# Scoring three query blocks in one run, and turning the second attention's weighted sum

## The reference

```python
# first block, 8 heads, 16 meta tokens ahead of the 512; mask by chunks of 64 positions
s = einsum('bqhmd,bkhmd->bhmqk', q, k)              # two maps m per head, 64 features each
p = softmax(where(mask, s, NEG_INF))
a = p[:, :, 0] - lam * p[:, :, 1]
o = einsum('bhqk,bkhe->bqhe', a, v)                 # then rms norm, gate
# second block, dsa_attention, 4 heads of 64 features, 128 keys selected for each query
p = softmax(where(valid, einsum('bqhd,bqkhd->bqhk', q, ks) * scale, -inf))
hC = einsum('bqhk,bqkhd->bqhd', p, vs)
out = concatenate([hA, hB, hC]) @ w_out
```

## Time and profile before

| what | value |
|---|---|
| runs | 1533.29, 1533.55, 1533.76 us |
| profiled execution | 1534.0 us, span of its instructions 1532.1 us |
| TensorE busy | 1520.7 us, 9994 passes |
| VectorE, ScalarE, GpSimd busy | 1101.7, 646.7, 55.4 us |
| DMA | 131.64 MB, 86 GB/s on average |
| granted TensorE clock | 1.000 on average |

### The profile page before, as it was taken

How to read it: one execution, slowest core, us unless ns; L and a number is a source line. 1 busy time by engine, 2 the same in 40 slices (tenths; PEclk the granted TensorE clock), 3 DMA queues, 4 the chain that set the end, 5 groups by cost and what they waited for, 6 DMA issues and landing times.

```text
span 1532.1 us, 25451 instructions
## 1 busy us (share of the span) xinstructions
PE 1520.7 (99%) x9994; PEld 1362.9 (89%) x9994; DVE 1101.7 (72%) x1550; ACT 646.7 (42%) x1015; POOL 55.4 (4%) x115
## 2 busy tenths in 40 slices
PE   9999999999999999999999999999999999999998
PEld 8999999999999999999988888878888888888887
DVE  5889888888655587777764458988748887887123
ACT  5224545555643434434334335744645333333122
POOL 0000111111000000000000020000000000000000
PEclk9999999999999999999999999999999999999999
DMA  6333222232233243232232443231132333332221
GB/s 180 83 93 100 56 72 68 57 83 56 56 102 92 83 110 82 82 109 82 66 94 81 115 109 83 57 83 42 56 110 56 110 101 91 89 103 96 110 83 55
DMA packets 235360, 131.64 MB, mean 86 GB/s; under 512 B 20985, under 2 KB 228741, under 8 KB 235285
## 3 DMA queue, kind: packets, MB, share of 16 engines
q1 hardware_dynamic: 234900, 130.40, 30.3%
q0 software_dynamic: 384, 0.20, 0.0%
HBM read 128.48 MB, written 2.10 MB: 85 GB/s over the span
## 4 chain that ended last, share of the span: by engine, by line
PE 91%; DVE 5%; ACT 2%; issue 0%; DMA 0%; SPq 0%; DVEq 0%; ACTq 0%
PE psP L726 32%; PE psS L726 25%; PE psP L791 8%; PE psS L1432 4%; PE psP L1432 4%; PE psP L748 4%; PE psP L1122 3%; PE psP L1300 1%; DVE conv L2170 1%; PE psS L1300 1%; PE psP L969 1%; DVE wl L2050 1%; PE psP L879 1%; PE psS L928 1%; PE psS L1189 1%; PE psP L956 1%
## 5 line engine op out<-in xcount | busy, mean ns | idle before, releaser
L2050 DVE TENSOR_TENSOR wl<-raw,wh 128x2048 fp32r<-128x2048 f32 x124 | 284.1, 2291 | 174.8 <-ACT wh L1487 173.4
L1487 ACT ACTIVATE wh<-raw 128x2048 fp32r<-128x2048 f32 x124 | 237.0, 1911 | 207.1 <-PE psS L1432 74.3
L726 PE MATMUL psP<-xh,wh 128*128 128x264 f32 (+3 forms) x1184 | 296.0, 312 | 1.2 <-DVE wl L2050 0.5
L726 PE MATMUL psP<-xl,wh 128*128 128x264 f32 (+3 forms) x1184 | 291.4, 309 | 0.0
L726 PE MATMUL psP<-xh,wl 128*128 128x264 f32 (+3 forms) x1184 | 290.3, 308 | 0.0
L726 PE MATMUL psS<-xh,wh 128*128 128x256 f32 (+2 forms) x880 | 210.3, 305 | 0.4 <-DVE hT L2079 0.4
L726 PE MATMUL psS<-xl,wh 128*128 128x256 f32 (+2 forms) x880 | 208.1, 303 | 0.0
L726 PE MATMUL psS<-xh,wl 128*128 128x256 f32 (+2 forms) x880 | 207.2, 302 | 0.0
L726 PEld LDWEIGHTS psP<-xh,wh 128*128 128x128 f32 x1184 | 192.2, 189 | 16.3 <-issue 2.2
L726 PEld LDWEIGHTS psP<-xl,wh 128*128 128x128 f32 x1184 | 192.7, 189 | 12.0 <-issue 0.2
L726 PEld LDWEIGHTS psP<-xh,wl 128*128 128x128 f32 x1184 | 192.2, 189 | 11.9
(11 more groups left out here) (483 smaller groups left out, 2429.7 us busy)
## 6 DMA issues: line engine op xcount, KB each, us to landing
raw<-in_w_in_dram SPq DMA_DIRECT2D x74, 512.0 KB, 4.9
raw<-in_w_up_dram SPq DMA_DIRECT2D x44, 512.0 KB, 4.6
raw<-in_ffn_up_dram SPq DMA_DIRECT2D x44, 512.0 KB, 4.9
raw<-in_ffn_down_dram SPq DMA_DIRECT2D x22, 512.0 KB, 3.9
raw<-in_w_out_dram SPq DMA_DIRECT2D x16, 512.0 KB, 4.7
raw<-in_w_down_dram SPq DMA_DIRECT2D x16, 384.0 KB, 3.6
raw<-in_w_down_dram SPq DMA_DIRECT2D x16, 320.0 KB, 4.0
raw<-in_w_conv_out_dram SPq DMA_DIRECT2D x8, 512.0 KB, 4.6
```

The source lines that it names most:

```text
L726: ins = mm(dst, W[:, s, half, k, 0:rows], Y[:, k, c0 + o:c0 + o + w], start=(k == 0 and p == 0), stop=(k == KT - 1 and p == 2))
L1487: fn(wh[:, n % 2], raw[:, n % 2], ACT.Copy).then_inc(s_hi, 1)
L2050: V.tensor_tensor(wl[:, n % 2], raw[:, n % 2], wh[:, n % 2].bitcast(f32), ALU.subtract).then_inc(s_lo, 1)
```

## The change

First part, head stage. Blocks 0, 1 and 2 are scored one after another; blocks 0 and 1 share two PSUM banks (`SCORE_COL`), so maxima and exponentials of block 0 wait for block 1's scores and maxima. Turn-back goes to the front of the pass. Outputs (and VectorE's variances, ScalarE's output copy) go behind part 0 in passes 2 to 7, and stay ahead of it in passes 8 and 9. Values, scores 3 and the transposes of blocks 0 and 1 together (`first_probs`) stand behind part 1. ScalarE's and VectorE's orders follow.

Second part, second attention. ScalarE divides the probabilities in place (`divide_probs`) before they are transposed. `weighted` is made once a block, with the 64 value columns standing and 128 columns of turned probabilities moving, two heads in the two halves of the PSUM partitions; its result is already by feature, so `osb`, `scale_outputs` and `attention_back` go. High and low parts are taken block by block out of that bank.

```diff
+SCORE_COL = (0, 160, 0)
...
+        def score_rows(t):
+
+            o = SCORE_COL[t]
+            return scores_ps[:, 2 * (t // 2):2 * (t // 2) + 2, o:o + PW[t]]
...
             def scores(a, t):
-                if a:
-                    pe.wait_ge(s_ex, 4 * a + (0, 0, 1, 3)[t])
-                elif t >= 2:
-                    pe.wait_ge(s_ex, t - 1 if t == 2 else 3)
+                if t == 3:
+                    pe.wait_ge(s_ex, 4 * a + 3)
+                elif a:
+                    pe.wait_ge(s_ex, 4 * a)
...
+            def first_probs(a):
+                pe.wait_ge(s_cb, 4 * a + 2)
+                pe.wait_ge(s_ac, 4 * a + 1)
+                for j, o in enumerate((PO[0], PO[1], PO[1] + 128)):
+                    ins = tr(psP[1][:, 0, 128 * j:128 * (j + 1)], prob[:, o + NM:o + NM + 128], ident[:])
+                ins.then_inc(s_at, 1)
...
             for h in range(NH + 2):
                 a, b, c = h - 1, h - 2, h - 3
+                if c >= 0:
+                    pe.wait_ge(s_ea, evacuated(2 * (N_HEAD + 2 * h) - 2)[1])
+                    turn_back(c, psP[0])
                 if b >= 0:
                     probs(b, 3)
                 if 0 <= a < NH:
                     scores(a, 0)
                     scores(a, 1)
-                if c >= 0:
-                    pe.wait_ge(s_ea, evacuated(2 * (N_HEAD + 2 * h) - 2)[1])
-                    turn_back(c, psP[0])
-                if b >= 0:
+                    scores(a, 2)
+                if h >= NH:
                     outputs(b)
...
                 part(h, 0)
-                if 0 <= a < NH:
-                    if h < NH:
-                        values(a)
-                    scores(a, 2)
-                    probs(a, 0)
+                if 0 <= b < NH - 2:
+                    outputs(b)
...
                 part(h, 1)
                 if 0 <= a < NH:
-                    probs(a, 1)
+                    if h < NH:
+                        values(a)
                     scores(a, 3)
+                    first_probs(a)
                 part(h, 2)
...
-            def weighted(i, load, h0, h1):
+            def weighted(i, load):
...
-                for h in range(h0, h1):
-                    o = 256 * (i % 2) + 64 * h
+                for f in range(2):
+                    o = 256 * (i % 2) + 128 * f
                     for j in range(t + 1):
-                        ins = mm(psP[1][:, 1, o:o + 64], PT[:, h, 128 * j:128 * (j + 1)], av[:, j, 64 * h:64 * (h + 1)],
-                                 start=(j == 0), stop=(j == t))
+                        for b in range(2):
+                            h = 2 * f + b
+                            ins = mm(psP[1][64 * b:64 * b + 64, 1, o:o + 128], av[:, j, 64 * h:64 * (h + 1)],
+                                     PT[:, h, 128 * j:128 * (j + 1)], start=(j == 0), stop=(j == t))
+                ins.then_inc(s_po, 1)
...
             def exps(a, t):
-                act.wait_ge(s_ma, 4 * a + t + 1)
+                act.wait_ge(s_ma, 4 * a + max(t, 1) + 1)
...
-            def scale_outputs(i):
+            def divide_probs(i):
+                t = BLOCKS[i]
+                act.wait_ge(s_pn, i + 1)
+                for h in range(AT_H):
+                    p = prt[t][:, h, :]
+                    fn(p, p, ACT.Copy, scale=att[:, 1, i, h:h + 1]).then_inc(s_pw, 1)
...
             values(0)
             attention_exps(0)
             values(1)
+            divide_probs(0)
             hi(n + 13)
...
             attention_exps(2)
-            scale_outputs(1)
+            attention_hi(1)
+            divide_probs(2)
             copy_probs(2, 6, 0, 1)
             hi(N_WO2)
...
             copy_probs(2, 9, 3, 4)
+            divide_probs(3)
             gelu(2)
             lru_hi(1)
+            attention_hi(2)
             copy_probs(3, 10, 0, 4)
...
             for h in range(NH + 2):
                 n, a, b, c = N_HEAD + 2 * h, h - 1, h - 2, h - 3
+                if c >= 0:
+                    gated(c, psP[0])
                 if 0 <= a < NH:
                     maxima(a, 0)
                     maxima(a, 1)
...
-                if b >= 0:
+                if h >= NH:
                     variances(b)
+                if 0 <= a < NH:
+                    maxima(a, 2)
                 taps(2)
                 if h == NH:
                     dve.wait_ge(s_lmc, 1)
                     centred(0, 4)
-                if 0 <= a < NH:
-                    maxima(a, 2)
+                if 0 <= b < NH - 2:
+                    variances(b)
...
             mask_logits(0)
             select(3, 8, 10)
+            invert_sums(0)
             mask_logits(1)
-            invert_sums(0)
             lo(n + 13)
-            select(3, 10, 13)
+            select(3, 10, 12)
+            invert_sums(1)
+            select(3, 12, 13)
+            attention_lo(0)
             scaled(lg[:, 0, :], 2 * (n + 12))
```

More of the change, by code:

```diff
@@ L926, in scores @@
                     if t < 3:
-                        bank = scores_ps[:, 2 * (t % 2) + m, :]
-                        mm(bank[:, 0:PW[t]], q, K[:, 0:PW[t]], start=True, stop=False)
+                        bank = score_rows(t)[:, m, :]
+                        mm(bank, q, K[:, 0:PW[t]], start=True, stop=False)
                         last.append(bank[:, PW[t] - 64:PW[t]])
@@ L1364, in _ @@
             turn(0, 1, 2, 4)
-            weighted(0, 0, 0, 2)
             lru_side(0, 2, 4)
-            weighted(0, 1, 2, 4)
+            weighted(0, 1)
             lru_side(0, 4, 8)
@@ L1856, in copy_probs, with attention_hi @@
                 fn(PT[:, h0:h1, 0:w], psP[1][:, 0, 0:w * (h1 - h0)].rearrange("p (h c) -> p h c", c=w), ACT.Copy).then_inc(s_pc, 1)
-            def scale_outputs(i):
+            def divide_probs(i):
[4 more added lines that the diff above has]
+                    fn(p, p, ACT.Copy, scale=att[:, 1, i, h:h + 1]).then_inc(s_pw, 1)
+            def attention_hi(i):
                 t = BLOCKS[i]
                 act.wait_ge(s_po, i + 1)
-                act.wait_ge(s_pn, i + 1)
-                for h in range(AT_H):
-                    o = 256 * (i % 2) + 64 * h
-                    ins = fn(osb[:, t, 64 * h:64 * (h + 1)], psP[1][:, 1, o:o + 64], ACT.Copy, scale=att[:, 1, i, h:h + 1])
-                ins.then_inc(s_pd, 1)
+                o = 256 * (i % 2)
+                fn(ch[:, 6:8, 128 * t:128 * (t + 1)], psP[1][:, 1, o:o + 256].rearrange("p (f q) -> p f q", f=2), ACT.Copy).then_inc(s_hc, 1)
             def gelu(g):
@@ L1959, in _ @@
             attention_exps(1)
-            scale_outputs(0)
+            attention_hi(0)
+            divide_probs(1)
             copy_probs(1, 2, 0, 1)
@@ L1975, in _ @@
             copy_probs(2, 9, 3, 4)
+            divide_probs(3)
             gelu(2)
             lru_hi(1)
+            attention_hi(2)
             copy_probs(3, 10, 0, 4)
             lru_hi(2)
-            scale_outputs(2)
             hi(N_WO2 + 1)
-            scale_outputs(3)
-            act.wait_ge(s_pb, TT)
-            for f in range(2):
-                fn(ch[:, 6 + f, :], scores_ps[:, f, :], ACT.Copy).then_inc(s_hc, 1)
+            attention_hi(3)
             hi(N_WO2 + 2)
@@ L2260, in _ @@
                     maxima(a, 1)
-                if c >= 0:
-                    gated(c, psP[0])
-                if 0 <= a < NH:
                     ratios(a, 0, 2)
@@ L2674, in _, with attention_lo @@
                                        ch[:, g, :].bitcast(f32), ALU.mult, ALU.subtract).then_inc(s_hl, 1)
+            def attention_lo(i):
+                t = BLOCKS[i]
+                tok = slice(128 * t, 128 * (t + 1))
+                o = 256 * (i % 2)
+                dve.wait_ge(s_hc, i + 1)
+                V.tensor_tensor(cl[:, 6:8, tok], psP[1][:, 1, o:o + 256].rearrange("p (f q) -> p f q", f=2),
+                                ch[:, 6:8, tok].bitcast(f32), ALU.subtract).then_inc(s_hcl, 1)
             mask_logits(0)
             select(3, 8, 10)
+            invert_sums(0)
             mask_logits(1)
-            invert_sums(0)
             lo(n + 13)
-            select(3, 10, 13)
+            select(3, 10, 12)
+            invert_sums(1)
+            select(3, 12, 13)
+            attention_lo(0)
             scaled(lg[:, 0, :], 2 * (n + 12))
@@ L2683, in _ @@
             mask_logits(2)
-            invert_sums(1)
             scaled(lg[:, 1, :], 2 * (n + 12) + 1)
+            invert_sums(2)
+            attention_lo(1)
             mask_logits(3)
-            invert_sums(2)
             lo(N_WO2)
@@ L2695, in _ @@
             lru_lo(1)
+            attention_lo(2)
             lru_lo(2)
             lo(N_WO2 + 1)
-            for f in range(2):
-                dve.wait_ge(s_hc, f + 1)
-                V.tensor_tensor(cl[:, 6 + f, :], scores_ps[:, f, :], ch[:, 6 + f, :].bitcast(f32), ALU.subtract).then_inc(s_hcl, 1)
+            attention_lo(3)
             lo(N_WO2 + 2)
```

93 lines of the change are left out of this document (37 added, 56 removed).

## The result

The changed kernel takes 1538.2 us (median of 8 runs, 1536.9 to 1540.9); the kernel before took 1533.7 beside it (8 runs, 1533.3 to 1534.0). The ratio is 1.0031, 95% interval 1.0023 to 1.0040: slower by 4.5 us. Forecast: +3.4 us, 1537.0, with 0.56 on slower. The profiled execution took 1537.8 us, its span 1536.0.

What follows compares the result with a forecast made beforehand. TensorE, busy 1520.7 of 1532.1 us, was taken as the bound. Own work -5.5, first head's waits -0.3, eighth +3.5, ninth +0.6, second attention's waits +5.1 gave +3.4: 1537.0 us, range 1532.8 to 1540.6.

Steps and rivals of the forecast that it cites:

- Scores in one run: Heads: block 2's scores join a run already in paired form, gaining 0.27 us a head, 2.2 us over eight.
- Rival 4: Inner heads: VectorE's loop is longer than a head, six heads by 0.3 to 0.7: 1539 to 1541 us; chance 0.09.
- First, eighth and ninth: Heads with changed waits on TensorE: first head net -0.3 us, eighth +3.5, ninth pass +0.6.
- Second attention: Own work -0.9 for dropped turn-back and -2.4 for the weighted sum, waits +5.1; k = 2 comes 1.8 us later.
- The column halves: Second attention's weighted sum: the two halves overlap, 40 pairs at 0.11 us plus entries and exits, -2.4 us.
- four entries and exits: Second attention's weighted sum: entering and leaving the paired form four times, at about 0.35 us each.
- Rival 1: Second attention: column halves don't overlap, blocks 2 and 3 add 1.7 + 0.4: 1539.1 us; chance 0.22.
- 2 (waits covered): Eighth head and second attention: ScalarE's chain is not the last, so waits are covered: 1527.7 us, faster; chance 0.08.
- 3 (one stage only): Waits of either the eighth head or the attention are smaller by half or more: 1533 to 1535.3 us; chance 0.19.

Runs made afterwards that it cites:

- e1: The change's head-stage hunks only, with the second attention of the kernel before: 1536.3 us, ratio 1.0017.
- e4: Changed kernel plus 18 matmuls whose result nobody reads between parts 0 and 1 of the eighth head: 1538.0 us.
- e2: The change's second attention only, with the heads of the kernel before: 1536.2 us, ratio 1.0015.
- e6: As e3, but the weighted sum's two heads of a pair run one after the other instead of alternating column halves: 1537.1 us, ratio 1.0023.
- e5: Changed kernel plus matmuls whose results nobody reads in each longer new wait, eighth head and second attention: 1536.7 us, ratio 1.0020.
- e11: As e10, with the high part of block 2's output ahead of the third gelu on ScalarE, low part likewise on VectorE: 1530.4 us, ratio 0.9980.
- e7: As e3, with ScalarE's and VectorE's queues in the second attention reordered and block 2's division on VectorE: 1534.7 us, ratio 1.0008.
- e10: As e8, with second attention's conversion ahead of the exponentials and projection to its end ahead of block 2's turn: 1531.9 us, ratio 0.9988.
- e3: Changed kernel with ScalarE emptying part 0 in the eighth head before the third square: 1534.9 us, ratio 1.0010.
- e8: As e7, with the eighth head's conversion of the second weights behind the copies that part 0 waits for: 1533.2 us, ratio 0.9996.
- e9: The change's heads with both eighth-head repairs (early emptying, later weight conversion) and the second attention of the kernel before: 1532.1 us, ratio 0.9989.

## Why the prediction was right

The sign, the size and the places came out; one cost was missing, and two terms of the second attention were wrong in size and happened to cancel.

**Scores in one run.** Forecast -0.27 a head. The inner head after, against the earlier trace rows:

```profile
303.30:335.66 32.36, 32.36 (x272) 30.55 (x271) 26.81 (x45) 17.26 (x45) 6.95 (x11) 1.00 0.24 67
```

32.36 for 32.63: right, and for the reason given. Block 2 stands right behind block 1's mask, and from that mask (328.87) to its own (329.65) it takes the 0.78 us of the forecast:

```profile
328.87 0.20 PE L939 MATMUL psS<-mkk,mki 64*128 64x64 bf16 x2
328.90 0.92 PE L932 MATMUL psS<-qkv 64*128 64x400 f32 x4
329.65 0.20 PE L939 MATMUL psS<-mkk,mki 64*128 64x64 bf16 x2
```

Rival 4 (VectorE's loop longer than a head) is out: TensorE doesn't wait in the inner heads.

**First, eighth and ninth.** Forecast waits: 2.4 ahead of part 1 in the eighth head, measured 2.44; 0.6 more for aTm in the ninth, measured 0.85 for the earlier trace rows's 0.3; 0.85 between parts 0 and 1 of the first head, measured 0.7. Ahead of part 0, 1.6 forecast, 1.36 + 0.43 measured. Sum of the heads: +1.6 forecast; +1.5 measured where the clock did not fall in part 1 (e1, e4: 924.2), +3.1 where it did.

**Second attention.** Forecast +1.8 at output product k = 2; there the distance from the logits went from 48.2 us (1060.21 to 1108.45) to 49.95 (1062.64 to 1112.59): +1.7. To the end it is +1.5 without a slow stretch, +3.0 with one (e2). The listed waits are 0.3 and 1.4 ahead of the first turns of blocks 0 and 2, 0.96, 0.2 and 0.2 for copies, 1.9 for the output product: 5.1, less 0.4 of old ones, where I had 5.1 net. Own work lost 3.1 in the weighted sum, where I had 2.4 (below). The waits, 4.7 where I had 5.1, and the 0.7 more of own work would have given +0.7 and not +1.8. That it came out at +1.7 is luck, a third error that I had not seen: the list counts a wait from the end of the last pass. The pass at 1073.10 is 0.40 long, but in a run such passes start every 0.235; the next, at 1074.45, is late by 1.12 us and not by the 0.96 listed. Over six waits that is 1 us.

**The column halves.** The mechanism held: the halves overlap, and a pair costs the 0.11 us that I took from the row halves (0.44 us for each 8 passes more). Mis-sized were the four entries and exits, 0.35 each in the forecast and 0.14 measured; that is the whole 0.7 by which the gain was too small: 4.4 + 0.6 = 5.0 us and not 5.8. Rival 1 is out, since the pairs overlap. Its price of 0.11 for a pass without overlap agrees with e6's first passes, but no run here has all 80 so. Of the two sentences that I had set against each other from the Trainium skill, *TensorE: Matmul & The Clock Gate, Part 3*, the one that outputs in different column groups run concurrently agrees with these pairs. The other, that a load overlaps running products only if the row group differs, is not borne out as I used it: all 80 passes use the same 128 rows, and they follow each other every 0.062 us on average with loads recorded at 0.137 each.

**What was missing: the clock.** The earlier trace rows show 1.000, and the kernel before has no wait over 0.5 us near the change, so I priced a wait at its own length. Here it costs more: each stretch at 1.2 GHz adds 1.5 to 1.7 us, and the changed kernel has two places for it. Without any it is 2.8 us over the kernel before (the one execution of e4 whose trace has none, 1536.3) to 3.3 (e5's median, with the fillers in it); its median is +4.5. So some 1.2 to 1.7 of the 4.5 us are the clock's, and the forecast's +3.4 is close to the kernel without them.

**Rivals.** 2 (waits covered) became true only with the repairs: e11, 1530.4, still above its 1527.7, since its list still has some 5 us of waits in the changed stages, none over 0.9. 3 (one stage only) is out by e1 and e2, which each lose about 1.4 us in their lowest groups.

## What to carry to other kernels

Where TensorE is 99% busy, an engine that was never the bottleneck becomes one as soon as its work is put into TensorE's chain. Here four copies in place (divisions of 1.7 to 2.6 us) and one conversion of 1.9 us decided over a change that saves TensorE some 6 us of passes; so for each moved instruction ask which chain will be the last one at the next hand-over, and after a repair ask it again (e7 and e10 each uncovered the next chain).

A wait on TensorE can cost its own length and then 1.5 to 1.7 us more of slow clock behind it, in part of the executions only. Times that fall into groups of a fixed distance are a hint, and matmuls whose result nobody reads, put into the wait, are the test.

Passes of 64 stationary columns pay when two halves of the array run at once: by itself such a pass took the same 0.11 us as one with 128 stationary and 64 moving columns. And an experiment that is to take an overlap away must be read in the trace for how much of it is gone: e6's 0.9 us is a lower bound.

## What the runs showed of the hardware

- The granted clock fell to 0.50 for 3.4 us, each time behind waits of TensorE: after 1.33 + 0.43 us (e1, from 369.7), after 1.36 + 0.43 and a further 2.44 (changed kernel, from 378.5), after the second attention's 1.45 and 1.95 (e2, e3), after 2.35 (e8). With the same waits filled (e5), or with none in the changed stages over 0.9 us (e9) or 1.5 (e10), all eleven executions lay within 1.3, 0.7 and 1.1 us.
- The same waits did not always bring it: e1, e2 and e3 have four, five and six of their executions in the lower group, and the traces of e4 and e6 (with the wait of 1.95) and e7 (with 2.35) show no slow stretch there. What decides in a single execution, no trace here shows.
- A slow stretch in part 0 of e1 cost nothing, since TensorE would have waited 1.5 us longer behind it.
- Passes with 64 stationary and 128 moving columns follow each other every 0.11 us in one column half and at 0.055 us in alternating halves (80 in 5.0 us with four entries and exits of 0.14); passes with 128 stationary and 64 moving columns every 0.11 us.
- With one head's passes behind the other's (e6) 32 passes took 2.50 us, where 32 at 0.11 would be 3.5: passes still overlapped. Which ones, the trace doesn't name.
